# Input projections of a fused two-block kernel: x in eight transfers, the small value projection as a turned tile, side work spread differently, branches in another order

## The reference

```
h     = rmsnorm(x, norm_mix_pre)
proj  = h @ w_in         # g_q g_k g_v g_low g_r | s_q s_k s_v | p_u | gates
y_a   = gla_mixer(g_q, g_k, g_v, g_low, g_r, ...) @ w_branch_gla
y_b   = swa_mixer(s_q, s_k, s_v, sinks)           @ w_branch_swa
y_c   = pool_mixer(p_u, pool_w, pool_scale)       @ w_branch_pool
merged = sigmoid(gates_0)*y_a + sigmoid(gates_1)*y_b + sigmoid(gates_2)*y_c
x = x + rmsnorm(merged @ w_out, norm_mix_post)
```

## Time and profile before

| | us |
|---|---|
| median of the runs | 1536.01 |
| the profiled execution, its own time | 1534.79 |
| its span, first to last instruction | 1533.0 |
| TensorE busy | 1453.6 (95%) |
| VectorE busy | 913.5 (60%) |
| ScalarE busy | 602.2 (39%) |
| mean granted TensorE clock | 0.975 |

### The profile page before, as it was taken

How to read it: one execution, slowest core, us unless ns; L and a number is a source line. 1 busy time by engine, 2 the same in 40 slices (tenths; PEclk the granted TensorE clock), 3 DMA queues, 4 the chain that set the end, 5 groups by cost and what they waited for, 6 DMA issues and landing times.

```text
span 1533.0 us, 17910 instructions
## 1 busy us (share of the span) xinstructions
PE 1453.6 (95%) x7120; PEld 1179.2 (77%) x7120; DVE 913.5 (60%) x1277; ACT 602.2 (39%) x908; POOL 171.3 (11%) x122
## 2 busy tenths in 40 slices
PE   6998989899999999999999999799999999988898
PEld 5776767678878788788888888567787888866687
DVE  5443756374442788726885377534455647888664
ACT  5231543533334523222223353334344544556451
POOL 3300010120222200000000120000002112211020
PEclk9999999999999999999999999899999999999899
DMA  6221312122344323432333242311124332211132
GB/s 215 73 65 41 97 56 64 48 70 64 101 124 151 97 71 108 124 97 82 97 97 114 93 126 63 103 39 58 55 69 151 96 103 94 69 42 54 44 124 69
DMA packets 36835, 134.37 MB, mean 88 GB/s; under 512 B 4224, under 2 KB 4880, under 8 KB 36240
## 3 DMA queue, kind: packets, MB, share of 16 engines
q1 hardware_dynamic: 36752, 133.23, 28.3%
HBM read 127.97 MB, written 5.24 MB: 87 GB/s over the span
## 4 chain that ended last, share of the span: by engine, by line
PE 72%; DVE 18%; ACT 6%; issue 3%; DMA 1%; POOL 1%; DVEq 0%; SPq 0%; ACTq 0%
PE ps L197 71%; DVE WL L151 4%; DVE CT L163 2%; DVE TT L163 1%; DVE TH L151 1%; ACT L194 1%; DVE PB L151 1%; DVE QK L163 1%; DVE SS L163 1%; DVE sm L169 1%; DVE CT L158 1%; ACT SS L194 1%; DVE HL L163 1%; ACT PH L181 1%; DVE gqks L151 1%
## 5 line engine op out<-in xcount | busy, mean ns | idle before, releaser
L197 PE MATMUL ps<-HH,WH 128*128 128x512 f32 x1208 | 494.2, 409 | 18.1 <-DVE WL L151 12.7
L197 PE MATMUL ps<-HH,WL 128*128 128x512 f32 x1208 | 476.4, 394 | 0.0
L197 PE MATMUL ps<-HL,WH 128*128 128x512 f32 x1208 | 476.0, 394 | 0.0
L151 DVE TENSOR_TENSOR WL<-raw,WH 128x1024 fp32r<-128x1024 f32 x222 | 281.7, 1272 | 75.5 <-ACT WH L181 74.8
L181 ACT CAST WH<-raw 128x1024 fp32r<-128x1024 f32 x222 | 231.4, 1043 | 148.8 <-PE ps L197 130.0
L197 PEld LDWEIGHTS ps<-HH,WH 128*128 128x128 f32 x1208 | 230.4, 191 | 74.8 <-issue 12.8
L197 PEld LDWEIGHTS ps<-HH,WL 128*128 128x128 f32 x1208 | 230.0, 190 | 50.2
L197 PEld LDWEIGHTS ps<-HL,WH 128*128 128x128 f32 x1208 | 230.6, 191 | 47.2 <-issue 2.0
L197 PE MATMUL ps<-PH,WH 128*128 128x512 f32 x426 | 171.8, 403 | 3.5 <-DVE PL L151 2.9
L151 POOL TENSOR_TENSOR SQS<-SQS,SQ 128x512 f32<-128x512 f32 x54 | 79.8, 1477 | 800.9 <-ACT SQ L194 800.0
L197 PE MATMUL ps<-PH,WL 128*128 128x512 f32 x426 | 168.2, 395 | 0.0
(11 more groups left out here) (205 smaller groups left out, 1502.5 us busy)
## 6 DMA issues: line engine op xcount, KB each, us to landing
raw<-in_wall SPq DMA_DIRECT2D x222, 512.0 KB, 3.6
X<-in_xT SPq DMA_DIRECT2D x8, 512.0 KB, 6.4
kept<-PW SPq DMA_DIRECT2D x2, 1536.0 KB, 7.6
PWR<-kept SPq DMA_DIRECT2D x2, 1536.0 KB, 7.6
out_T<-X SPq DMA_DIRECT2D x8, 256.0 KB, 2.1
pe<-in_pT SPq DMA_DIRECT2D x2, 512.0 KB, 5.2
pt<-in_pT SPq DMA_DIRECT2D x2, 512.0 KB, 4.1
DM<-in_dm SPq DMA_DIRECT2D x1, 640.0 KB, 4.1
```

The costliest lines, as they stand in the source:

```text
L151: return self.put(None if self.e is None else self.e.tensor_tensor(out, x, y, op))
L197: return self.put(None if self.e is None else self.e.matmul(out, l, r, start=start, stop=stop, skip_group_check=True))
```

## The change

SP transfers the eight columns of the first norm's gain by themselves, then X in eight transfers of one slice, with raw units 0, 1 and 2 behind slices 0, 3 and 5, and the rest of cv behind slice 7. ACT begins with a square root of a few ones, takes WH of units 0 to 3 right behind HH 0, 1, 3 and 5, and waits for cv only before the norm; POOL still waits for cv before its first sum. DVE takes WL of unit 3 in this loop. sv becomes an ordinary tile ahead of the sq tiles, scaled by DVE into TT, turned by four transposes (`sv_turn`, in the middle of sq 0) and copied to SVT by ACT. The pool's side steps run at rate 2 beside sk, sv, sq 0 and sq 1; swa at 1.7 from glow to the end of branch 0, gla at 1.7 in the rest of branch 0 and at 2 in the tiles r and in branch 1. A gla pair has 21 steps. `tokens` waits for WL of a unit when the first token block reaches it. The r tiles come between branch 0 and branch 1 and write RG (in the place of PL 8 to 11, after the mark "pooled"); the product with on_t and the split (GH, GL) go into gla_side. The order of the weights in memory and the calls of all five programs follow.

```diff
     def tokens(self, names, ops, width):
         n = len(ops)
-        held = [self.block(width // P) for _ in ops]
+        first = self.blk
+        held = [self.block(width // P, ready=False) for _ in ops]
         for t, name in enumerate(names):
             out = self.fill(self.next_bank(), name)[:, 0:width]
             for k, (h, l, sig, key) in enumerate(ops):
                 wh, wl, u = held[k]
+                if t == 0:
+                    self.wait_ge(self.S.wlo, "unit", (first + k * width // P) // 8)
...
+        RG = at("RG", [P, 4, T], F32, ploff + 16384)
+        GH, GL = PH[:, 8:12, :], PL[:, 0:4, :]
...
+            def sv_turn():
+                s = p.fill(SB[4], ("svt",))
+                p.wait_ge(S.dve, "sv")
+                for t in range(4):
+                    p.transpose(s[:, t * P:(t + 1) * P], tt_("sv")[:, t * P:(t + 1) * P], ident)
+                p.then_inc("svt", free("T", ("sv",)))
+                yield
...
             p.side.append(pool)
+            p.rate = 2
             p.tile(("sk",), H_mix)
+            p.tile(("sv",), H_mix)
+            p.soon.append(sv_turn())
             for j in range(4):
                 p.tile(("sq", j), H_mix)
-            p.tokens([("sv", t) for t in range(4)], H_mix, P)
-            p.finish(pool)
+            p.rate = 1.7
             swa = swa_side()
             p.side.append(swa)
             p.tile(("glow",), H_mix)
+            p.finish(pool)
             for pr in range(2):
                 p.tile(("gq", pr), H_mix)
                 p.tile(("gk", pr), H_mix)
             p.tokens([("gv", t) for t in range(4)], H_mix, T)
             p.side.append(gla_side())
-            p.rate = 2.4
             branch(0, O_pool)
+            p.mark("pooled")
             p.finish(swa)
+            p.rate = 2
+            for h in range(4):
+                p.tile(("r", h), H_mix)
             branch(1, O_swa)
             p.drain()
-            for h in range(4):
-                p.tile(("r", h), H_mix)
             branch(2, O_gla)
...
+                def output(h):
+                    v.wait_ge(S.act, "ga hi", h)
+                    v.wait_ge(S.dve, "ga in", h)
+                    v.tensor_tensor(GL[:, h, :], RG[:, h, :], GH[:, h, :].bitcast(F32), SUB).then_inc(("ga", h))
...
+                        if e_:
+                            output(h - 1)
+                        v.wait_ge(S.dve, "silu2", ("r", h))
+                        v.wait_ge(S.dve, "on", h)
+                        v.tensor_tensor(RG[:, h, :], RG[:, h, :], on_t[:, h, :], MUL).then_inc(("ga in", h))
                         yield
+                    output(2 * pr + 1)
+                    yield
...
+                v.take("TH", t, wait=False)
+                v.wait_ge(S.pe, *t)
+                v.wait_ge(S.pe, "mark", "pooled")
+                v.tensor_tensor(RG[:, h, :], ps(*t), RS, MUL).then_inc(("th in", t), free(t))
+                v.wait_ge(S.act, "tanh", t)
+                v.wait_ge(S.dve, "th in", t)
+                v.scalar_tensor_tensor(RG[:, h, :], th_(*t), 1.0, RG[:, h, :], ADD, MUL).then_inc(("silu2", t), free("TH", t))
+            branch(1, 4)
...
+            a.wait_ge(S.dve, "ones")
+            a.activation(sm[:, 80:84], ones[:, 0:4], ACT.Sqrt).then_inc("warm")
+            a.wait_ge(S.gain, "gain")
             for k in range(8):
-                a.wait_ge(S.cvec, "cvec")
-                a_high(a, "mix", k, "mix_pre", HH, S.x[k // 2], "x")
+                a_high(a, "mix", k, "mix_pre", HH, S.x[k], "x")
+                if k in (0, 1, 3, 5):
+                    a.high()
                 a_square(a, "mix", k, X[:, k, :], None)
-                if k in (1, 3, 5):
-                    a.high()
+            a.wait_ge(S.cvec, "cvec")
...
         def sp_program(s):
-            s.dma_start(cv, a_in["cvec"]).then_inc("cvec", sig=S.cvec, by=16)
-            for i in range(4):
-                s.dma_start(X[:, 2 * i:2 * i + 2, :], a_in["xT"][:, 2 * i:2 * i + 2, :]).then_inc("x", sig=S.x[i], by=16)
-                if i < NRAW:
-                    s.load()
+            def load_x(k):
+                s.dma_start(X[:, k, :], a_in["xT"][:, k, :]).then_inc("x", sig=S.x[k], by=16)
+
+            s.dma_start(cv[:, 0:8], a_in["cvec"][:, 0:8]).then_inc("gain", sig=S.gain, by=16)
+            load_x(0)
+            s.load()
+            for k in (1, 2, 3):
+                load_x(k)
+            s.load()
+            for k in (4, 5):
+                load_x(k)
+            s.load()
+            for k in (6, 7):
+                load_x(k)
+            s.dma_start(cv[:, 8:NCOL], a_in["cvec"][:, 8:NCOL]).then_inc("cvec", sig=S.cvec, by=16)
...
```

More of the change, by code:

```diff
@@ L389, in fill, with block @@
         return self.psum[:, bank, :]
-    def block(self, n=1):
+    def block(self, n=1, ready=True):
         u, k = divmod(self.blk, 8)
@@ L1513, in dve_program @@
             v.side.append(pool)
+            v.rate = 2
             v.tile(8)
@@ L1516, in dve_program @@
             v.tensor_tensor(SKT, ps("sk"), RS, MUL).then_inc("sk", free("sk"))
+            v.tile(8)
+            v.take("T", ("sv",))
+            v.wait_ge(S.pe, "sv")
+            v.tensor_tensor(tt_("sv"), ps("sv"), RS, MUL).then_inc("sv", free("sv"))
             for j in range(4):
@@ L1520, in dve_program @@
                 v.scalar_tensor_tensor(SQT[:, j, :], ps("sq", j), 0.125, RS, MUL, MUL).then_inc(("sq", j), free("sq", j))
-            for t in v.tokens(8, P):
-                pass
-            v.finish(pool)
+            v.rate = 1.7
             swa = swa_side()
@@ L1526, in dve_program @@
             v.tile(8)
+            v.finish(pool)
             v.wait_ge(S.pe, "glow")
@@ L1539, in dve_program @@
             v.side.append(gla_side())
-            v.rate = 2.4
             branch(0, 4)
             v.finish(swa)
-            branch(1, 4)
-            v.drain()
+            v.rate = 2
             for h in range(4):
@@ L2031, in act_program, with sv_turn @@
             a.side.append(pool)
-            for _ in range(5):
-                a.tile(8)
[L2034 to L2038, removed]
+            a.rate = 2
+            def sv_turn():
+                a.wait_ge(S.pe, "svt")
+                a.copy(SVT.rearrange("p a b -> p (a b)"), ps("svt")).then_inc("sv", free("svt"))
+                yield
+            a.tile(8)
+            a.tile(8)
+            a.soon.append(sv_turn())
+            for _ in range(4):
+                a.tile(8)
+            a.rate = 1.7
             swa = swa_side()
             a.side.append(swa)
-            for _ in range(5):
+            a.tile(8)
+            a.finish(pool)
+            for _ in range(4):
                 a.tile(8)
@@ L2047, in act_program @@
             a.side.append(gla_side())
-            a.rate = 2.4
             branch(0, 4)
             a.finish(swa)
+            a.rate = 2
+            for h in range(4):
+                a.tile(8)
+                t = ("r", h)
+                a.wait_free(S.before.get(("TH", t)))
+                a.wait_ge(S.dve, "th in", t)
+                a.activation(th_(*t), RG[:, h, :], ACT.Tanh, scale=0.5).then_inc(("tanh", t))
             branch(1, 4)
             a.drain()
[L2053 to L2056, removed]
-                a.copy(PH[:, h, :], tt_("r", h)).then_inc(("ga hi", h))
             branch(2, 4)
@@ L2280, in gla_side @@
                         yield
-                    for _ in range(12):
+                    for _ in range(13):
                         yield
@@ L2307, in pool_program @@
             g.side.append(pool)
-            for _ in range(5):
+            g.rate = 2
+            for _ in range(6):
                 g.tile(8)
-            for t in g.tokens(8, P):
-                pass
-            g.finish(pool)
+            g.rate = 1.7
             swa = swa_side()
             g.side.append(swa)
-            for _ in range(5):
+            g.tile(8)
+            g.finish(pool)
+            for _ in range(4):
                 g.tile(8)
@@ L2319, in pool_program @@
             g.side.append(gla_side())
-            g.rate = 2.4
             branch(0, 4)
             g.finish(swa)
+            g.rate = 2
+            for h in range(4):
+                g.tile(8)
             branch(1, 4)
             g.drain()
-            for h in range(4):
-                g.tile(8)
             branch(2, 4)
@@ L2356, in sp_program @@
             s.first(8, 4)
-            for _ in range(5):
-                s.tile(8)
-            for t in s.tokens(8, P):
-                pass
-            for _ in range(5):
+            for _ in range(11):
                 s.tile(8)
@@ L2364, in sp_program @@
                 pass
[L2365 to L2372 removed]
+            for b in range(3):
+                for _ in range(8):
+                    s.tile(8)
+                    s.tile(4)
+                if b == 0:
+                    for h in range(4):
+                        s.tile(8)
             s.wait_mark("gla", 1)
```

50 lines of the change are left out of this document (20 added, 30 removed).

## The result

The changed kernel takes 1501.62 us (1499.87 to 1502.41, four runs) against 1535.81 us (1532.66 to 1536.23) of the kernel before on the same chip: ratio 0.978, 95% interval 0.9763 to 0.9797. The profiled execution took 1501.85 us with a span of 1500.0, 33.0 less than before's 1533.0. At the first tile of branch 2 the lead is already 32.7 us (391.56 before, 358.88 after, the first `by` group of that branch in either timeline), so what follows looks at the mixing stage alone.

The account below looks back on a forecast made before the run. TensorE, busy 1453.6 of 1533.0 us, was taken as the bound, with waits and low-clock spells in the mixing stage. Terms 3.6 + 4.6 + 4.2 + 5.0 + 6.9 - 1.0 = 23.3 us gave 1512.7 us, range 1503 to 1526.

Parts of the forecast that it names:

- a, the start: Kernel start: raw 0 lands earlier and TensorE starts at 9.0 us instead of 12.70; 3.6 us gained (2.0 to 4.8).
- step e: GLA levels: more matmuls between gup and level 1 shorten the qks waits, fewer slow spells; 6.9 us gained (2.0 to 11).
- Rival 4: Start: the split fails, raw 0 lands no earlier than 8 us, a is 0; 1516 us, chance 0.06.
- b: sv as a tile plus four transposes instead of 96 matmuls of 128 columns; 4.6 us gained (4.2 to 4.8).
- c: The pool's end: waits around the last pm groups mostly go at rate 2; 4.2 us gained (2.5 to 5.2).
- Rival 2: Pool: POOL and DVE block each other, pm 3 waits 3 to 4 us, c about 0; 1517 us, chance 0.10.
- d: gv: the 5.25 us wait for WL shrinks to 1.15 us and the clock recovers; 5.0 us gained (3.0 to 6.2).
- Rival 1: GLA waits: chains decide, not spacing; tile work lengthens them, e, d and a shrink; 1520.7 us, chance 0.16.
- f: Costs: moved r tiles no longer cover GLA's tail, window attention steps are denser; -1.0 us (0 to -5).
- Rival 5: Glow to gv and branch 0: window attention starves TensorE over 26 steps; slower, 1559 us, chance 0.04.
- Rival 3: Both long GLA waits nearly go, no slow spells, e 11 and f 0; 1507.6 us, chance 0.09.

Follow-up runs that it names:

- (5): Changed kernel with the old start (cv whole and first, X in four transfers, HH and squares ahead of WH 0): 1504.16 us, ratio 0.9805.
- experiment 6: Changed kernel with sv computed by tokens again, 96 matmuls of 128 columns in place of the turned tile: 1505.98 us, ratio 0.9812.
- experiments 7: Changed kernel with rate 2.4 instead of 2 in the r tiles and branch 1: 1514.8 us, ratio 0.9866.
- experiment 8: Changed kernel with one more empty side step behind each gup and rate 2.1 instead of 2 in r tiles and branch 1: 1501.68 us, ratio 0.9784.
- experiments 2: Changed kernel with the eager wait for WL in `tokens` put back as before: 1508.66 us, ratio 0.9833.
- (1): Kernel before with only the lazy wait: `tokens` waits for a unit's WL at the first matmul that reads it: 1528.71 us, ratio 0.9963.
- experiment 11: Kernel of experiment 8 with GpSimd's half of each level's subtraction done on VectorE: 1501.68 us, ratio 0.9774.
- experiment 3: Kernel before with two more empty side steps behind each gup and rate 2.65 instead of 2.4 in the branches: 1525.75 us, ratio 0.9945.

## Why the prediction was wrong

The direction held, and what steps a to e were meant to do shows in the traces; the failure is of size, most of it in step e. At the head of branch 2 the lead is 32.7 us, 9.4 more than the sum. By steps, with what the traces give, waits and clock together:

- **a, the start (3.6; about 2.4).** First matmul at 8.87, forecast 9.0; a cast of WH 0 at 6.43. Two losses were not in the sum: TensorE's slow intervals at the start are nine instead of five (0.8 us), and the norm's wait for sm is 1.3 instead of 0.7 us, which varies between executions. Put back (5), the start costs 2.5 us. The small first transfer landed 1.6 us after its issue, about 2.1 us before x's first lands, so the rule that the prediction cites from the Trainium skill (DMA: Bandwidth & Descriptors, Specifications), on rows under 512 bytes, cost nothing that shows. Rival 4 is out.
- **b (4.6).** Supported: 4.4 by experiment 6; the turn waited 0.2 us.
- **c (4.2; 4.6).** The 1.0 us kept as loss was not lost: pm groups at 44.71, 51.06, 58.29 and 64.64 us stand without a wait. But not all of the 4.2 us were a wait: 2.89 us were, and the spell took 1.7, 0.8 of it in the pm group itself. Rival 2 did not happen here. No run undid this part alone.
- **d (5.0; 6.7).** No wait is left, where 1.15 was to stay. The step's error was the list on VectorE: the scores come a step earlier than I placed them, and the fourth unit's WL is done at 113.25, before 113.86 when it is read. The wait of 5.25 us and its spell of 1.4 are gone.
- **e (6.9; 12.1), the step that failed.** "The waits fall to 2.7 and 5.3 us" was 2.01 and 2.59, and "of the four slow spells I take 1.5 as gone" was three, worth 3.2 us and not 1.5. (The two falls were also mis-added: 4.93 to 2.7 and 6.19 to 5.3 are 2.2 and 0.9, not 2.4 and 1.0.) The sum of the waits for qks and at the transposes fell by 8.9 us, not 5.4. Most of the miss is pair 1: its chain is 10.52 us, not 12.74, and I had written "in which nothing changes". One of the two table loads ahead of the logarithm (1.28 us) and one WL left it. In the kernel before they stood here (in the changed kernel only the load at 278.62 us is left of them):

```profile
291.07 1.28 ACT L194 ACT_TABLE_LOAD   x1
...
293.02 1.28 ACT L194 ACT_TABLE_LOAD   x1
...
297.77 1.22 DVE L151 TENSOR_TENSOR WL<-raw,WH 128x1024 fp32r<-128x1024 f32 x1
```

  Rival 1 took the chain to be stretched by tile work; it is, by 3.7 us, but in experiments 7 and 8. The changed kernel happens to meet the short one: that part of the gain is luck.
- **f (-1.0; +0.6).** No such wait appeared, and one of 0.6 us for PTT went. Rival 5 is out.

The differences are -1.2, 0, +0.4, +1.7, +5.2 and +1.6; with 1.5 us that the spell at the norm was shorter, which no step named and which varies between executions, they make 9.2 of the 9.4 us. The clock is in most of them. It was priced at 3.5 us (1.0 in c, 1.0 in d, 1.5 in e), since one spell was counted as five intervals, 1.0 us; it gave 7.0. Even all high ends together (32.0 us) stay below the measured 34.2: e passed its own end of 11, d its end of 6.2. Rival 3, which comes nearest in time, had only 0.09, and its reason did not come true either, as 4.6 us of the long GLA waits are left.

What is argued and not shown: why an equal wait is followed by a spell in one execution and by none in another. The traces of experiments 2 and 5 show that it is so; no run here separates what decides it. Nor does any run move the r tiles back, so their move has no price of its own.

## What to carry to other kernels

Price a wait of TensorE by its length and the stretch behind it: here 4.6 us of wait taken out were worth 5.4 us of time (1), and 3.57 us put in cost 7.0 (2), each give or take 2 or 3 us. Before a difference of 1 us between two traces is called the work of an edit, look at a stretch that the edit does not touch: the spells there differ as well. Spacing a side chain pays until the chain itself changes: before giving it another step, write down what each engine of it has just ahead at that place, an addition on GpSimd, a table load, a WL. A rate is a phase as well as a density, so try two neighbours of it: 2, 2.1 and 2.4 gave 1501.6, 1501.7 (with one more step) and 1514.8 us.

## What the runs showed of the hardware

- Transfers of 128 rows of 32 bytes (4 KB) landed 1.6 us after issue, ahead of 256 KB (3.2 us for x's first) and 512 KB (4.8).
- A load of ScalarE's table, 1.28 us, stood ahead of the wait where the activation waits for one engine (280.11 in experiment 11) and behind a wait where it waits for two (285.13 in experiment 8).
- VectorE's two subtractions of 256 columns take 0.75 us alone and 1.85 us beside a GpSimd addition of 2.20 us.
- A wait of 2.0 us of TensorE had no slow stretch behind it in the changed kernel's trace (clock 1.00), and one in the traces of experiments 2 and 5 (0.96 both).
- In one program, behind one wait of 2.89 us, TensorE made five slow intervals in one execution and eight in another (the kernel before, experiment 3).
